# Row loads, first-layer entry and side-job steps rearranged in a trunk kernel with pooled gMLP mixer and 7-product MLP

## Chip, cores, metric

One Trainium2 chip, all 8 NeuronCores; every core runs the same program on its own eighth of the tokens, with no exchange between cores. The metric is the device time of the slowest core, in microseconds. Cores 0 to 3 are one die, 4 to 7 the other.

## What is computed

For each token row `x` (width 1024, float32 in memory): `h = RMSNorm(x)*g1`; `z = h @ w_in` (1536 columns: 512 pooling, 512 `u`, 512 `v`); pooling mixer: trailing means over 2, 4, 8 or 16 tokens minus the token, then a 128x128 map per group and a scale; gMLP mixer: `gelu(u) * (W_s gelu(v) + b)` over chunks of 128 tokens; `x += [pool | gmlp] @ w_out`; `x += relu(RMSNorm(x)*g2 @ w_up)**2 @ w_down` with 4096 hidden columns; a final RMSNorm gives `y`. Small outputs are the last pooling rows and `v` of the sample chunk. Each core has 33 tiles of 128 token rows, and 16 halo rows in front.

## The kernel before

**Tiles and groups.** The 33 tiles form nine groups (`GROUPS`, L18): group 0 has 3 tiles, group 1 has 2, groups 2 to 8 have 4. A ring of nine slots `XS` holds the float32 rows; tile t of the core lies in slot t mod 9. So the rows of group i+2 go into slots that rows of group i leave: row 0 of group i+2 into the slot of the last row of group i-1, rows 1, 2 and 3 into those of rows 0, 1 and 2 of group i. A row is loaded by `load_x` (L402 to L405), squared and summed on ACT (`sq`, L349, into `JUNK`), its inverse root taken on POOL (`rs`, L354 to L358), multiplied on DVE into `HB` (`apply`, L361 to L366), transposed on PE (L373) and copied by ACT (L377). At the end `final_sq`, `final_rs` and `final_out` (L770 to L787) do the same for the last norm, and `final_out` stores the row to `yall`.

**Order by hand.** Nothing is reordered by a compiler. `add(engine, ...)` appends to one of five in-order engine programs and works out the semaphore waits (from L49). A DMA is issued from the SP, ACT or POOL program, and an issue whose wait is not yet met holds up everything behind it in that program. Row loads in the middle of the kernel, row stores, the `rs` pairs and the loads and stores of raw MLP weights all stand in the POOL program.

**Stages.** (1) Entry (L790 to L892): rows of groups 0 and 1, `WAU` (four pieces, `w_in` for pooling and u), `WV`, `w_out`, small constants; PE runs 24 spare matmuls (L562), then transposes and projections `WI_au` (L419), `WI_v` (L440). Float32 weights are converted to bf16 on the way in, by DMAs in the POOL program. (2) Two rounds c = 0, 1 of pairs (L909 to L976): groups 0 and 1 go through the MLP with raw weights in a ring of five 1 MB buffers (`RING`); `pair_UP` (L580) is one step each, then step u(k) is the k-th of 20 `pair_DN` steps (L594). Beside them DVE forms weight sums (`wsum`, L602, L608) for the fast products, which are stored to scratch by the SP program, and the four sets of raw weights are stored too. (3) Group 2 (`plain`) has 32 `UP` steps (L619), then 28 DN steps d(0) to d(27) (L757). (4) Groups 3 to 8: the up product as seven half-size products (L668): 23 steps, `US2(0)`, then `US1(b+1)`, `US3(b)` (L705, L709), `US2(b+1)` (L697) in turn; called the UP stage here, with steps 0 to 22; then 28 DN steps. `US3`'s copy on ACT (L705) and its two subtractions on DVE (L709) must be done before PE may write the same banks again, two products later.

**Side jobs.** Each main step has side jobs, appended after it: `side(k, ...)`. The tables `ws`, `e1`, `tn` and `dn` hold their steps. In stage 4, with i the group whose MLP runs and j = i+1: `tn` holds the steps in the UP stage for j's norm (`sq`, `ap`, `tr`), projections (`v`, `au`), pooling (`pl`), the last norm of rows 2 and 3 of group i-1 (`fq`, `fo`) and the load of row 3 of j (`lx`); `dn` holds those in the DN stage, `lx=(3, 22, 25)` among them: row 0 of group i+2 at d(3), and rows 1 and 2 at d(22) and d(25), one step behind the `final_out` of rows 0 and 1 of group i at d(21) and d(24). The loads overwrite the slot that this `final_out` has just given to its store.

Of the kernel before, what the change touches and what calls it, by code (L numbers as in the profile page):

```python
# [117 lines left out]
def build_nc():  # L118
# [36 lines left out]
    with contextlib.ExitStack() as es:  # L155
# [106 lines left out]
        def schedule(P, order, record):  # L262
# [550 lines left out]
            spare(24)  # L813

            sq("1", 3, XH, [("X", 8)], 16)
            rs("1", 3, 4, 16)
            hb_h = next_hb()
            add("dve", lambda e: e.scalar_tensor_tensor(out=HB[hb_h][0:16], in0=XH, scalar=RS["1"][0:16, 3:4], in1=G1B[0:16],
                                                        op0=ALU.mult, op1=ALU.mult),
                reads=[("X", 8), ("RS", "1", 3), "G1B"], writes=[("HB", hb_h)])  # L820
            N1_sq(0, 0)
            rs("1", 0, 1)
            N1_apply(0, 0)
            norm_T(HB[hb_h], [("HB", hb_h)], HT[:, :, 0:16], ["HMh"], 16)
            for n in range(1, 3):
                N1_sq(0, n)
                rs("1", n, n + 1)
                N1_apply(0, n)
                N1_T(0, n - 1)
# [313 lines left out]
```

How the kernel before makes its waits and increments, by code:

```python
        def run(engname, e, final=False):  # L77
            waited = {}
            pe_ch = prog.engchan["pe"]
            for fn, waits, chn in prog.ops[engname]:
                need = {}
                for w in waits:
                    if engname == "pe" and w.chan is pe_ch:
                        continue
                    if w.val > need.get(w.chan, 0):
                        need[w.chan] = w.val
                for ch, v in need.items():
                    if waited.get(ch, 0) >= v:
                        continue
                    e.wait_ge(ch.sem, v)
                    waited[ch] = v
                ins = fn(e)
                ins.then_inc(chn.sem, chn.inc)
            if final:
                for ev in final_waits:
                    e.wait_ge(ev.chan.sem, ev.val)
```

## Time and profile before

| what | us |
|---|---|
| median of 3 runs | 1239.54 (1237.45 to 1247.37) |
| the profiled execution, own time | 1246.71 |
| its slowest core (1), first to last instruction | 1245.2 |
| its spans over the 8 cores | 1212.4 to 1245.2 |
| PE matmul busy on core 1 | 1179.2 |

The profiled execution is one execution with all cores recorded; 1.5 us of its time lie outside the span. Its own time is 7.2 us above the median of the other three. Times in timeline rows run from the first instruction of that core. A timeline row gives start, length, engine, line, operation, names, and in brackets how long the engine sat idle before it and what ended that.

### The profile page before, as it was taken

What the parts mean: (1) busy time and instruction counts of PE and PEld (TensorE: products, weight loads), DVE (VectorE), ACT (ScalarE), POOL (GpSimd) and SP (SyncE); (2) the same over time, 40 slices, a digit from 0 to 9 for tenths busy, and PEclk for the clock granted to TensorE, in tenths of its full rate; (3) what the DMA queues carried; (4) which work ended last, traced back from release to release, by engine and by line L of the source; (5) the groups of instructions that cost most, each with busy time, mean ns of one, the idle gap of its engine ahead of it and who ended that gap; (6) DMA issues with size and microseconds to landing.
All of it is one profiled execution on the core that took longest, in us unless ns stands there. A gap on an engine that the chain in (4) does not pass through costs nothing.

```text
span 1245.2 us, 21470 instructions; the slowest of 8 cores (1212.4 to 1245.2 us)
## 1 busy us (share of the span) xinstructions
PE 1179.2 (95%) x7412; PEld 701.2 (56%) x7412; DVE 803.9 (65%) x1164; ACT 438.2 (35%) x678; POOL 156.8 (13%) x303
## 2 busy tenths in 40 slices
PE   6889999988999999999999999997999999999996
PEld 2547456533444577446754577445764576547842
DVE  3564545386567675867587675865778575976773
ACT  3446022323410454134530364132640365233401
POOL 3111000113000220022100220021100220011001
PEclk7999999999899989999999999998999999999998
DMA  9996798989995895769767794769856896869993
GB/s 197 167 212 168 210 249 208 209 327 311 331 310 196 261 311 176 255 228 314 270 228 235 263 332 165 267 217 305 281 199 224 252 371 135 299 201 324 307 330 130
DMA packets 64907, 310.41 MB, mean 249 GB/s; under 512 B 9872, under 2 KB 9936, under 8 KB 44064
## 3 DMA queue, kind: packets, MB, share of 16 engines
q1 hardware_dynamic: 48992, 239.35, 57.9%
q0 software_dynamic: 15664, 69.15, 21.8%
q8 instruction: 62, 1.02, 0.3%
q10 hardware_dynamic: 144, 0.52, 0.2%
q14 instruction: 45, 0.37, 0.1%
HBM read 277.90 MB, written 53.31 MB: 266 GB/s over the span
## 4 chain that ended last, share of the span: by engine, by line
PE 73%; DMA 17%; DVE 3%; issue 3%; ACT 2%; POOL 1%; DVEq 0%; POOLq 0%; SPq 0%; ACTq 0%
PE ps L757 23%; PE ps L668 20%; PE ps L538 9%; PE ps L419 9%; DMA scr_up<-RING 5%; DMA yall<-XS 5%; PE ps L440 4%; PE ps L619 3%; PE ps L594 3%; DMA RING<-w_mlp 2%; DMA RING<-scr_up 2%; PE ps L373 2%; DMA XS<-xall 1%; ACT JUNK L350 1%; DMA scr_um<-RING 1%
## 5 line engine op out<-in xcount | busy, mean ns | idle before, releaser
L757 PE MATMUL ps<-RING,ST 128*128 128x512 bf16 x1120 | 256.9, 379 | 0.3 <-DVE ST L730 0.3
L350 ACT ACTIVATE JUNK<-XS 128x1024 bf16<-128x1024 f32 (+1 forms) x100 | 105.5, 1055 | 315.3 <-DVE XS L543 228.9
L668 PE MATMUL ps<-H2T,RING 128*128 128x256 bf16 x1536 | 184.1, 278 | 16.6 <-DVE ST L709 15.0
L757 PEld LDWEIGHTS ps<-RING,ST 128*128 128x128 bf16 x1120 | 108.7, 98 | 126.5 <-issue 1.7
L668 PEld LDWEIGHTS ps<-H2T,RING 128*128 128x128 bf16 x1536 | 152.2, 100 | 47.8 <-issue 20.1
L767 DVE TENSOR_TENSOR XS<-XS,ps 128x512 f32<-128x512 f32 x140 | 95.8, 685 | 75.3 <-PE ps L757 70.8
L668 PE MATMUL ps<-SB,RING 128*128 128x256 bf16 x1152 | 138.8, 273 | 3.9 <-DMA RING<-scr_um 2.2
L668 PEld LDWEIGHTS ps<-SB,RING 128*128 128x128 bf16 x1152 | 111.3, 98 | 20.4 <-issue 5.6
L719 ACT ACTIVATE ST<-ST 128x1024 bf16<-128x1024 bf16 x96 | 101.4, 1056 | 54.9 <-DVE ST L709 50.5
L419 PE MATMUL ps<-HT,WAU 128*128 128x512 bf16 (+2 forms) x512 | 118.0, 379 | 1.4 <-ACT HT L377 1.4
L709 DVE TENSOR_TENSOR ST<-PQ,ps 128x512 bf16<-128x512 f32 x96 | 61.7, 684 | 64.7 <-ACT PQ L705 37.5
L757 PE MATMUL ps<-RING,SB 128*128 128x512 bf16 x448 | 101.4, 379 | 0.0
L357 POOL TENSOR_SCALAR SS<-SS 128x1 f32<-128x1 f32 (+1 forms) x66 | 20.9, 317 | 607.8 <-ACT JUNK L350 606.5
L419 PEld LDWEIGHTS ps<-HT,WAU 128*128 128x128 bf16 x512 | 50.7, 99 | 55.1 <-issue 4.4
L543 DVE TENSOR_TENSOR XS<-ps,XS 128x512 f32<-128x512 f32 x66 | 45.4, 688 | 46.4 <-PE ps L538 44.7
L594 PE MATMUL ps<-RING,ST 128*128 128x512 bf16 x320 | 73.2, 385 | 1.4 <-DVE XS L599 1.4
L697 DVE TENSOR_TENSOR ST<-ps,PQ 128x512 bf16<-128x512 f32 x96 | 63.2, 686 | 15.1 <-PE ps L668 15.1
L757 PEld LDWEIGHTS ps<-RING,SB 128*128 128x128 bf16 x448 | 43.1, 98 | 48.3
L619 PE MATMUL ps<-H2T,RING 128*128 128x512 bf16 x256 | 58.4, 390 | 6.7 <-DMA RING<-scr_up 6.7
L783 DVE SCALAR_TENSOR_TENSOR XS<-XS,RSf,GFB 128x1024 f32<-128x1024 f32 (+1 forms) x34 | 42.1, 1249 | 26.7 <-POOL RSf L358 26.7
L705 ACT ACTIVATE PQ<-ps 128x512 f32<-128x512 f32 x48 | 28.7, 597 | 85.3 <-PE ps L668 75.1
L714 DVE SCALAR_TENSOR_TENSOR ST<-ST 128x1024 bf16<-128x1024 bf16 x48 | 58.4, 1216 | 0.0
(107 smaller groups left out, 1421.6 us busy)
## 6 DMA issues: line engine op xcount, KB each, us to landing
RING<-scr_dn SPq DMA_DIRECT2D x98, 1024.0 KB, 6.3
RING<-scr_um SPq DMA_DIRECT2D x120, 512.0 KB, 7.8
RING<-scr_up SPq DMA_DIRECT2D x48, 512.0 KB, 8.9
RING<-w_mlp POOLq DMA_DIRECT2D x16, 1024.0 KB, 14.8
yall<-XS POOLq DMA_DIRECT2D x29, 512.0 KB, 8.4
RING<-scr_wo SPq DMA_DIRECT2D x14, 1024.0 KB, 5.8
XS<-xall POOLq DMA_DIRECT2D x24, 512.0 KB, 7.9
scr_up<-RING POOLq DMA_DIRECT2D x8, 1024.0 KB, 14.1
```

Source lines behind the costliest of these rows:

```text
L350: add("act", lambda e: e.activation(out=JUNK[0:np_], in_=ap, func=AF.Square, scale=1.0 / 32, accum_out=SS[kind][0:np_, j:j + 1]), reads=re ...
L419: i_ = e.matmul(bank(fb)[:, 0:h0 + T], lhsT=WAU[:, m, k, :], rhs=rhs, start=(k == 0), stop=(k == 7))
L538: i_ = e.matmul(bank(fb)[:, :], lhsT=mix(i, k, n * 128, (n + 1) * 128), rhs=W[:, k, :], start=(k == 0), stop=(k == 7))
L594: i_ = e.matmul(bank(ub)[:, :], lhsT=HID[h](j0 + kk, n * 128, (n + 1) * 128), rhs=RING[s][:, kk, :], start=(kk == 0), stop=(kk == 7))
L619: i_ = e.matmul(bank(ub)[:, :], lhsT=RING[s][:, k, (m % 4) * 128:(m % 4 + 1) * 128], rhs=H2T[:, k, :], start=(k == 0), stop=(k == 7))
L668: i_ = e.matmul(bank(ub)[:, u * 256:(u + 1) * 256], lhsT=RING[s][:, h * 4 + k, c0 + u * 128:c0 + (u + 1) * 128], rhs=op[:, k, :], start=(f ...
L697: add("dve", lambda e, o=o, pb=pb: e.tensor_tensor(out=o, in0=v2(bank(pb)), in1=v2(PQ[b % 2][:, 0:512]), op=ALU.subtract), reads=[("PQ", b ...
L709: add("dve", lambda e, o=o, pb=pb: e.tensor_tensor(out=o, in0=v2(PQ[b % 2][:, 0:512]), in1=v2(bank(pb)), op=ALU.subtract), reads=[("PQ", b ...
L714: add("dve", lambda e: e.scalar_tensor_tensor(out=ST[:, m:m + 2, :], in0=ST[:, m:m + 2, :], scalar=0.0, in1=ST[:, m:m + 2, :], op0=ALU.max ...
L719: add("act", lambda e, fn=fn: e.activation(out=ST[:, m2:m2 + 2, :], in_=ST[:, m2:m2 + 2, :], func=fn), writes=st_res(m2 * 512, (m2 + 2) * ...
L757: i_ = e.matmul(bank(ub)[:, :], lhsT=lh(kk), rhs=RING[s][:, kk, :], start=(c == 0 and kk == 0 and M not in CONT), stop=(c == 1 and kk == 7 ...
L767: add("dve", lambda e, x=x, op_=op_: e.tensor_tensor(out=x, in0=x, in1=bank(ub)[:, :], op=op_), writes=[("BANK", ub), xres(i, rb * 2 + n)])
```

## The change

1. Entry. The first `WAU` piece waits for row 0 of group 0 instead of the halo rows, and stands behind the halo's `rs` in the POOL program; the other three pieces stand behind the `rs` of row 0. The three squares of group 0 go in front of all transposes and copies in the ACT program. The loads of group 1's two rows wait for `WAU` piece 2 (tensor rows m = 2, 3) instead of row 2 of group 0; `PSC`, and behind it in the SP program `PWF`, `BB` and `G2B`, waits for the last piece.
2. Pairs. Weight sum 4 from u(12) to u(11), weight sum 3 from u(14) to u(16), with the release of their ring buffers, in both rounds; the transposes of group 2's second norm one step earlier, u(4, 5, 7, 8).
3. Group 2's UP stage: the square of row 2 of group 3 from step 19 to 21. (`us=` in the new table is read nowhere, and `lx=(8, ...)` gives the old step.)
4. Groups 3 to 8: rows 1, 2 and 3 of group j are loaded in the UP stage at steps 1, 3 and 7; before, rows 1 and 2 at d(22) and d(25) of the DN stage before it, and row 3 at step 6. The `gate` jobs move from d(5, 5, 7, 7) to d(4, 4, 6, 6).

```diff
-            for m in (0, 2, 4, 6):
-                add("pool", lambda e, m=m: e.dma_start(out=WAU[:, m:m + 2], in_=w_au[:, m:m + 2]),
-                    reads=[("X", 8)] if m == 0 else [], writes=[("WAU", m), ("WAU", m + 1)], dma=f"wau{m}")
+            def load_au(m, lead):
+                add("pool", lambda e: e.dma_start(out=WAU[:, m:m + 2], in_=w_au[:, m:m + 2]),
+                    reads=lead, writes=[("WAU", m), ("WAU", m + 1)], dma=f"wau{m}")
...
+            sq("1", 3, XH, [("X", 8)], 16)
+            rs("1", 3, 4, 16)
+            load_au(0, [("X", 0)])
...
+            for n in range(3):
+                N1_sq(0, n)
+            rs("1", 0, 1)
+            for m in (2, 4, 6):
+                load_au(m, [])
+            N1_apply(0, 0)
+            norm_T(HB[hb_h], [("HB", hb_h)], HT[:, :, 0:16], ["HMh"], 16)
+            for n in range(1, 3):
+                rs("1", n, n + 1)
+                N1_apply(0, n)
+                N1_T(0, n - 1)
             for n in range(2):
                 add("sp", lambda e, n=n: e.dma_start(out=xap(1, n), in_=xall[(3 + n) * 128:(4 + n) * 128, :]),
-                    reads=[("X", 2)], writes=[xres(1, n)], dma=f"xldsp{slot_x(1, n)}")
-            add("sp", lambda e: e.dma_start(out=PSC[:], in_=pool_scale[:, :]), writes=["PSC"], dma="su5")
+                    reads=[("WAU", 2)], writes=[xres(1, n)], dma=f"xldsp{slot_x(1, n)}")
+            add("sp", lambda e: e.dma_start(out=PSC[:], in_=pool_scale[:, :]), reads=[("WAU", 6)], writes=["PSC"], dma="su5")
...
-                ws = dict(w=(5, 6, 10, 12, 14))
+                ws = dict(w=(5, 6, 10, 11, 16))
...
-                    e1 = dict(... na=(2, 3, 4, 5), nt=(5, 6, 8, 9), ...)
+                    e1 = dict(... na=(2, 3, 4, 5), nt=(4, 5, 7, 8), ...)
...
-                        side(8, L(load_x, j, n))
-                    tn = dict(sq=(15, 17, 19, 21), ...)
+                        side(tn["lx"][n], L(load_x, j, n))
+                    tn = dict(sq=(15, 17, 21, 21), ... us=(7, 7, 7, 7), lx=(8, 8, 8, 8))
...
-                    tn = dict(... fq=(0, 0), fo=(1, 7), lx=6)
+                    tn = dict(... fq=(0, 0), fo=(1, 7), lx=(1, 3, 7))
...
-                        side(tn["lx"], L(load_x, j, 3))
+                        for n in range(3):
+                            side(tn["lx"][n], L(load_x, j, n + 1))
...
-                dn = dict(... lx=(3, 22, 25), gt=(5, 5, 7, 7), ...)
+                dn = dict(... lx=3, gt=(4, 4, 6, 6), ...)
...
-                        side(d(dn["lx"][0]), L(load_x, i + 2, 0))
+                        side(d(dn["lx"]), L(load_x, i + 2, 0))
...
-                        if i + 2 < NG:
-                            side(d(dn["lx"][1 + n]), L(load_x, i + 2, n + 1))
```

## Rows read from the trace of the kernel before

**Rows 1.** The page: head and busy time by engine.
```profile
span 1245.2 us, 21470 instructions; the slowest of 8 cores (1212.4 to 1245.2 us)
PE 1179.2 (95%) x7412; PEld 701.2 (56%) x7412; DVE 803.9 (65%) x1164; ACT 438.2 (35%) x678; POOL 156.8 (13%) x303
```

**Rows 2.** Spans and mean granted clock of three of the cores.
```profile
core 1: 1245.2 us, clock 0.979
...
core 3: 1232.9 us, clock 0.985
...
core 7: 1212.4 us, clock 0.988
```

**Rows 3.** Core 1, five UP stages, one and the sum: length, busy (count), clock, DMA, GB/s.
```profile
844.90:924.90 80.00, 72.99 (x578) 55.61 (x577) 49.57 (x67) 38.70 (x55) 10.26 (x19) 0.96 0.75 253
...
sum 384.90, PE 365.63 PEld 277.43 DVE 249.24 ACT 194.60 POOL 51.40; mean PE 73.13 PEld 55.48 DVE 49.85 ACT 38.92 POOL 10.28
```

**Rows 4.** Core 7: the sum of the same five stages.
```profile
sum 362.20, PE 359.73 PEld 274.68 DVE 249.31 ACT 194.23 POOL 51.48; mean PE 71.95 PEld 54.94 DVE 49.86 ACT 38.85 POOL 10.30
```

**Rows 5.** Core 3: the sum of the same five stages.
```profile
sum 370.10, PE 361.03 PEld 274.15 DVE 249.27 ACT 194.16 POOL 51.53; mean PE 72.21 PEld 54.83 DVE 49.85 ACT 38.83 POOL 10.31
```

**Rows 6.** Core 1, waits of PE from 400 to 1100 us: total, times, longest.
```profile
PE ps L668 <- DVE ST L709: 15.0, 5, 7.0
```

**Rows 7.** Core 7, waits of PE from 400 to 1100 us: the same line.
```profile
PE ps L668 <- DVE ST L709: 0.3, 1, 0.3
```

**Rows 8.** Core 1, timeline of POOL, end of group 5's DN stage.
```profile
837.61 0.63 POOL L786 DMA_DIRECT2D yall<-XS  x1
...
850.23 0.54 POOL L786 DMA_DIRECT2D yall<-XS  x1
861.45 0.53 POOL L404 DMA_DIRECT2D XS<-xall  x1 [10.68 <-DMA yall<-XS]
```

**Rows 9.** Core 1, timeline of DVE and of PE just behind it.
```profile
863.09 1.29 DVE L783 SCALAR_TENSOR_TENSOR XS<-XS,RSf,GFB 128x1024 f32<-128x1024 f32 x1 [7.86 <-POOL RSf L358]
...
865.12 4.93 PE L668 MATMUL ps<-H2T,RING 128*128 128x256 bf16 x32 [7.01 <-DVE ST L709]
```

**Rows 10.** Core 7, timeline of ACT and POOL, the same place.
```profile
835.17 0.63 POOL L786 DMA_DIRECT2D yall<-XS  x1
...
841.43 1.06 ACT L350 ACTIVATE JUNK<-XS 128x1024 bf16<-128x1024 f32 x1
...
846.16 1.05 ACT L350 ACTIVATE JUNK<-XS 128x1024 bf16<-128x1024 f32 x1
```

**Rows 11.** Core 7, row loads issued from 400 to 1100 us, issue to landing.
```profile
DMA to landing us min/median/max: 5.5/9.1/9.8
```

**Rows 12.** Core 1, row stores issued from 400 to 1100 us, issue to landing.
```profile
DMA to landing us min/median/max: 5.9/8.5/11.2
```

**Rows 13.** Core 1, entry: timeline of SP and PE.
```profile
16.84 1.07 SPq L805 DMA_DIRECT2D XS<-xall  x2
...
23.20 7.13 PE L419 MATMUL ps<-HT,WAU 128*128 128x400 bf16 x27 [1.37 <-ACT HT L377]
...
41.17 5.32 PE L419 MATMUL ps<-ST,WAU 128*128 128x256 bf16 x32 [1.26 <-ACT ST L377]
```

**Rows 14.** Core 1, DMA issues from 16.8 to 17.5 us: KB each, median us to landing.
```profile
XS<-xall SPq DMA_DIRECT2D x2, 512.0 KB, 12.4
```

**Rows 15.** Core 1, pieces of the chain that ended last, from 84 to 260 us.
```profile
88.21 16.55 DMA scr_up<-RING
...
156.08 1.73 PE ps L594 x8
```

**Rows 16.** Core 1, timeline of POOL and PE, rounds c = 0 and c = 1.
```profile
180.17 0.53 POOL L307 DMA_DIRECT2D RING<-w_mlp  x1 [8.34 <-DMA scr_dn<-RING]
...
252.64 0.61 PE L373 MATMUL ps<-IDB,HB 128*128 128x128 bf16 x8 [3.75 <-DVE HB L364]
```

**Rows 17.** Core 1, DMA issues from 160 to 162 us.
```profile
scr_dn<-RING SPq DMA_DIRECT2D x1, 1024.0 KB, 18.7
```

More of the change, by code:

```diff
@@ L799, in schedule @@
             add("pool", lambda e: e.dma_start(out=IDB[:], in_=ident[:, :]), writes=["IDB"], dma="su0")
-            for m in (0, 2, 4, 6):
-                add("pool", lambda e, m=m: e.dma_start(out=WAU[:, m:m + 2], in_=w_au[:, m:m + 2]),
-                    reads=[("X", 8)] if m == 0 else [], writes=[("WAU", m), ("WAU", m + 1)], dma=f"wau{m}")
+            def load_au(m, lead):
+                add("pool", lambda e: e.dma_start(out=WAU[:, m:m + 2], in_=w_au[:, m:m + 2]),
+                    reads=lead, writes=[("WAU", m), ("WAU", m + 1)], dma=f"wau{m}")
             add("sp", lambda e: e.dma_start(out=INVC[:], in_=invc[:, :]), writes=["INVC"], dma="su6")
+            spare(24)
+            sq("1", 3, XH, [("X", 8)], 16)
+            rs("1", 3, 4, 16)
+            load_au(0, [("X", 0)])
+            hb_h = next_hb()
+            add("dve", lambda e: e.scalar_tensor_tensor(out=HB[hb_h][0:16], in0=XH, scalar=RS["1"][0:16, 3:4], in1=G1B[0:16],
+                                                        op0=ALU.mult, op1=ALU.mult),
+                reads=[("X", 8), ("RS", "1", 3), "G1B"], writes=[("HB", hb_h)])
+            for n in range(3):
[9 more added lines that the diff above has]
+                N1_T(0, n - 1)
             for n in range(2):
                 add("sp", lambda e, n=n: e.dma_start(out=xap(1, n), in_=xall[(3 + n) * 128:(4 + n) * 128, :]),
-                    reads=[("X", 2)], writes=[xres(1, n)], dma=f"xldsp{slot_x(1, n)}")
-            add("sp", lambda e: e.dma_start(out=PSC[:], in_=pool_scale[:, :]), writes=["PSC"], dma="su5")
+                    reads=[("WAU", 2)], writes=[xres(1, n)], dma=f"xldsp{slot_x(1, n)}")
+            add("sp", lambda e: e.dma_start(out=PSC[:], in_=pool_scale[:, :]), reads=[("WAU", 6)], writes=["PSC"], dma="su5")
             add("sp", lambda e: e.dma_start(out=PWF, in_=pool_wt[:, :, :]), writes=["GFB"], dma="su7")
@@ L812, in schedule @@
             add("sp", lambda e: e.dma_start(out=G2B[:], in_=g2.partition_broadcast(128)), writes=["G2B"], dma="su3")
[L813 to L829, printed above, removed]
             N1_T(0, 2)
@@ L960, in schedule @@
                 else:
-                    e1 = dict(v=(1, 3), pl=(0, 1, 2, 3), gt=(8, 8, 9, 10), wo=(14, 15, 16, 17, 18, 19, 20, 21), nq=(21, 22, 23, 24), rs=(23, 23, 25, 25), na=(2, 3, 4, 5), nt=(5, 6, 8, 9), fq=(16, 17, 18), fo=(19, 19, 19))
+                    e1 = dict(v=(1, 3), pl=(0, 1, 2, 3), gt=(8, 8, 9, 10), wo=(14, 15, 16, 17, 18, 19, 20, 21), nq=(21, 22, 23, 24), rs=(23, 23, 25, 25), na=(2, 3, 4, 5), nt=(4, 5, 7, 8), fq=(16, 17, 18), fo=(19, 19, 19))
                     for n in range(2):
@@ L1005, in schedule @@
                 if plain:
+                    tn = dict(sq=(15, 17, 21, 21), ap=(18, 20, 22, 24), tr=(23, 27, 27, 30), v=(36, 37, 39, 39), au=(31, 31, 33, 34, 35, 36, 37, 38), pl=(34, 36, 38, 39), us=(7, 7, 7, 7), lx=(8, 8, 8, 8))
                     side(0, *[L(final_sq, 1, n) for n in range(2)], L(final_rs, 0, 2))
@@ L1008, in schedule @@
                     for n in range(4):
-                        side(8, L(load_x, j, n))
-                    tn = dict(sq=(15, 17, 19, 21), ap=(18, 20, 22, 24), tr=(23, 27, 27, 30), v=(36, 37, 39, 39), au=(31, 31, 33, 34, 35, 36, 37, 38), pl=(34, 36, 38, 39))
+                        side(tn["lx"][n], L(load_x, j, n))
                 else:
-                    tn = dict(sq=(2, 5, 7, 11), ap=(3, 6, 9, 12), tr=(5, 8, 11, 14), v=(6, 11, 14, 19), au=(15, 16, 18, 18, 20, 21, 23, 24), pl=(18, 18, 21, 22), fq=(0, 0), fo=(1, 7), lx=6)
+                    tn = dict(sq=(2, 5, 7, 11), ap=(3, 6, 9, 12), tr=(5, 8, 11, 14), v=(6, 11, 14, 19), au=(15, 16, 18, 18, 20, 21, 23, 24), pl=(18, 18, 21, 22), fq=(0, 0), fo=(1, 7), lx=(1, 3, 7))
                     for n in (2, 3):
@@ L1016, in schedule @@
                     if j < NG:
-                        side(tn["lx"], L(load_x, j, 3))
+                        for n in range(3):
+                            side(tn["lx"][n], L(load_x, j, n + 1))
                 d = lambda k: d0 + k
-                dn = dict(s1=(0, 1, 2, 3), s7=(5, 5, 8, 9), s2=(10, 10, 11, 11), s6=(11, 11, 13, 12), sm=(12, 12, 13, 13), fq=(18, 20), fo=(21, 24), lx=(3, 22, 25), gt=(5, 5, 7, 7), wo=(10, 11, 12, 13, 14, 15, 16, 17), nq=(14, 15, 16, 17), na=(16, 16, 17, 18), nt=(17, 18, 19, 21), es=(25, 25, 26, 27, 27), u1=25)
+                dn = dict(s1=(0, 1, 2, 3), s7=(5, 5, 8, 9), s2=(10, 10, 11, 11), s6=(11, 11, 13, 12), sm=(12, 12, 13, 13), fq=(18, 20), fo=(21, 24), lx=3, gt=(4, 4, 6, 6), wo=(10, 11, 12, 13, 14, 15, 16, 17), nq=(14, 15, 16, 17), na=(16, 16, 17, 18), nt=(17, 18, 19, 21), es=(25, 25, 26, 27, 27), u1=25)
                 if plain:
```

## The prediction

> **What bounds the kernel now.** I read the page first: PE is busy 1179.2 of 1245.2 us on the slowest core [rows 1]. So only two things can move the time: the roughly 66 us in which PE has no matmul, and the speed of the matmuls. The spans by core come next: the same program takes 1212.4 us on core 7 and 1245.2 on core 1 [rows 2]. The metric is the slowest core, so I ask where cores 1 and 7 part. A table by stretches gives it: the five UP stages of groups 3 to 7 sum to 384.9 us on core 1, 362.2 on core 7 and 370.1 on core 3 [rows 3 to 5]. That is 22.7 us of the 32.8 between cores 1 and 7, and 7.9 for core 3. The last ten arise before group 2's DN stage ends.
>
> The waits of PE in that part name the place: 15.0 us in 5 times on core 1, one per stage, for DVE's subtraction L709; 0.3 us on core 7 [rows 6, 7]. 22.7 is more than 15.0 because a long wait also costs clock: the worst stage (80.0 us) has a mean granted clock of 0.96 against the full 2.4 GHz [rows 3].
>
> The timelines give the chain behind it. POOL issues row 0's store at 837.61. The only instruction between this and row 1's store is the load of row 1, which overwrites the slot being stored, and row 1's store goes out only at 850.23. The next load stands 10.68 us for that store, until 861.45 [rows 8]. Behind these in POOL's program stand the inverse roots of the last norm of rows 2 and 3. DVE waits 7.86 us for them, starts that multiplication at 863.09, and only then comes L709, for which PE waited 7.01 us, to 865.12 [rows 9]. Stores take 8.5 us in the median and up to 11.2 [rows 12]; two in series decide whether the roots come late. A core with quick DMAs slips through, one with slow ones stalls.
>
> **The change part by part.**
>
> (a) Row loads out of d(22) and d(25). In the new order POOL issues both stores, the four small instructions of two roots, row 2's store, and only then the load of row 1; its slot's store is then some 18 us old, so nothing is waited for. The double wait goes from all five boundaries. Gain on core 1: its sum comes down to core 7's, at most 22.7 us; on core 3 at most 7.9. What is late next is the row itself. On core 7 row 2's store went out at 835.17, so row 1's load goes out 0.6 us behind, or up to 2 us earlier since its root was itself held back: 834 to 836. With the median landing of 9.1 us [rows 11] the row is there at 843 to 845. Its square stood at 841.43 [rows 10]: ACT now waits 2 to 3.5 us. Row 2's load goes one root pair later, 836 to 837.5, lands at 845 to 847, and its square stood at 846.16 [rows 10]: about in time. Row 3's load moves behind one more step and one more store in POOL's program and keeps four steps, as row 1 has; I price it like row 1. Behind a waiting square on ACT stand two passes of the squared ReLU, the evacuation of `V` and the next `US` copy; behind its root on DVE the next `PQ` sum. PE needs these banks only two products later. From below the cost is nothing (all slack). From above it is the whole lateness, 3.5 twice, times 1.5 for the clock (22.7 over 15.0, [rows 3, 4, 6]): 10.5 us per boundary. I take 1.3, near the lower end, as a copy held 1 to 1.5 us still meets the bank in time and core 7 took similar shifts with 0.3 us of PE wait [rows 7]. Five boundaries: +6.5 us on every core.
>
> (b) Entry. Row 2 of group 0 arrives at 16.8 us on core 1 (the SP issue at 16.84 waited for it), and projections start at 23.20 [rows 13]. Without weights beside them the rows should come by 12 to 13, the three squares run without a transpose copy between them, and projections start near 18.5: 4 to 5 us earlier. Three DMA issues of 0.5 us now stand in front of the second root, inside this. But the loads of group 1's rows leave not at 16.84 but when the second weight piece lands, about 20, and take 12.4 us in the median of the pair [rows 14], the second longer. So that row comes near 35, and with square, root, multiply, transposes and copies of 1 to 1.3 us each the second projection block starts near 40.5 against 41.17 [rows 13], on quick cores perhaps 0.5 us later. What is won is given back. And both sit before a DMA chain: the first scratch store of raw weights takes 16.55 us, 88.21 to 104.8 [rows 15], since it stands behind a backlog of weights, whose volume the change leaves alone. If all 4.7 us survived it would be -4.7; if the second row is late and lets PE cool, +2. I take 0.
>
> The Trainium skill (DMA: Bandwidth & Descriptors, section Issuing engines are not separate DMA queues) says that DMAs of all issuing engines run on the same 16 engines and interleave. By that rule, splitting or delaying pieces changes only who is served first and the entry's sum stays 0, as taken; no run here shows it yet.
>
> (c) Weight sums. Sum 4 goes one step forward, sum 3 two steps back, which with the projections between them is up to 7 us of PE work (four times 8 matmuls of 1.73 us, [rows 15]). In round 0 sum 3's store is on the chain: POOL's load at 180.17 waits 8.34 us for it [rows 16], and the store takes 18.7 us [rows 17]. It takes that long because it stands behind two earlier megabytes in SP's queue, which drain whether it is issued at 161 or 168. So 0 to 2 us, up to 7 if it isn't so; I take 0.5, within (d)'s rounding. DVE work is the same, in another place.
>
> (d) Transposes at u(4, 5, 7, 8). In round 1 PE stands 3.75 us at the fourth transpose, until 252.64, for a product on DVE that stands behind a weight sum waiting for a raw load [rows 16]. That load is set by DMA. One step earlier PE meets the same late operand with one pair step (8 matmuls, 1.73 us [rows 15]) more still to do. Cost 1.7 us, from below 0 on a core where the load is early. Taken +1.7 on all cores.
>
> (e) Square at step 21 in group 2, and the gates one step earlier in DN: the same instructions in another order, in DN stages whose length did not differ between cores; DVE's gate work (eight passes of 0.7 us) lies beside PE's DN matmuls. If that cover failed it would be a microsecond per group. Taken 0.
>
> **Sum.** Against the profiled execution: core 1 gives 1245.2 - 22.7 + 6.5 + 1.7 = 1230.7; core 3 gives 1232.9 - 7.9 + 6.5 + 1.7 = 1233.2, and becomes the slowest. Plus 1.5 us outside the span: 1234.7, 12 us under 1246.7. But the profiled execution was 7.2 us above the median of the three runs, and part of that is surely the very stall that goes. I give half of it to the stall and half to the rest, so the forecast stands 3.3 us under 1234.7: 1231.4, 0.7% under 1239.54.
>
> **Rivals.**
> - The new waits take the place of the old: the late rows hold ACT, then DVE, then PE in each of five boundaries, on all cores alike, quick ones too. For it: a landing of 9.1 us against about 7 us of room. Against: two products of slack. It decides against the change from 3.7 us per boundary on (core 3: 1225.0 + 1.7 + 5 x 3.7 = 1245.2). At 6 us: 1225.0 + 1.7 + 30 + 1.5 = 1258, against the median about 1254. Slower.
> - The slack covers the rows entirely and the entry's gain survives: 1231.4 - 6.5 - 2 = 1223. For it: core 7 shows that lateness of 1 to 2 us is swallowed. Against: the DMA chain behind the entry.
> - Sum 3's later store shifts the raw-weight chain by its whole 7 us: 1231.4 + 7 = 1238, no measurable change. For it: the load waits for exactly that store. Against: the queue in front of it.
> - The change does not reach the slowest core, because some core is slow by ring loads and clock, not by this stall, in most runs: 1239.
>
> **How the numbers follow.** Forecast 0.50 (own range 1226 to 1237), new waits 0.13, chain shift 0.12, all slack 0.20, not reached 0.05. A measurement here tells about 1% from no change: 1227.1 and 1251.9. Faster by over 1%: most of the slack case and a tenth of the forecast, 0.25. Slower: the new waits beyond 5 us per boundary (0.08) and what I have not seen (0.02), 0.10. The rest 0.65. The range, 1222 to 1243, leaves out the heavy end of the new waits and little else.
>
> **What would show it right or wrong.** Right: no POOL wait at row loads from 400 us on, PE's wait for L709 near 0 to 1 us per boundary on every core, ACT waits of 1 to 3 us at the squares of rows 1 and 3, UP stages of 73 to 74 us on all cores, cores closer together. In the entry: projections at 18 to 19 us, then a PE gap before the second block near 40 us. The fourth transpose of round 1 waits 5 to 6 us. Wrong: UP stages of 76 us and more on core 7 (new waits), a load after sum 3's store later than 182 us, or an equal spread of the cores as before.

## The result, and the profile after the change

The changed kernel takes 1249.21 us in the median of 19 runs, the kernel before, run beside it, 1239.54 in the median of 19. The ratio is 1.0082, 95% interval 1.0065 to 1.0100: slower by 0.8%, where 0.7% faster was forecast, and above the range of 1222 to 1243. Some executions of either kernel are much slower, with a lower granted clock on one die; the ratio leaves them out, so it isn't quite the quotient of the medians. The profiled execution took 1252.26 us, 5.5 more than that of before.

The page of the profile after, cut to the head, PE's busy time and the chain that ended last (by line):

```profile
span 1250.7 us, 21476 instructions; the slowest of 8 cores (1234.2 to 1250.7 us)
...
PE 1179.1 (94%) x7412; PEld 699.9 (56%) x7412; DVE 803.7 (64%) x1164; ACT 437.5 (35%) x678; POOL 152.7 (12%) x303
...
PE ps L757 26%; PE ps L668 17%; PE ps L538 8%; PE ps L419 8%; DMA XS<-xall 4%; PE ps L594 4%; DMA scr_up<-RING 4%; PE ps L619 3%; PE ps L440 3%; DMA RING<-scr_um 3%; PE ps L580 3%; PE ps L373 2%; DMA RING<-w_mlp 2%; DMA scr_dn<-RING 1%; DMA scr_um<-RING 1%
```

PE's busy time is what it was [rows 1]. What is new is a 4% share of `XS<-xall` in the chain: landings of row loads now stand on it. Spans and mean granted clock of the fastest core and of the slowest:

```profile
core 3: 1234.2 us, clock 0.982
...
core 6: 1250.7 us, clock 0.979
```

Before they ran from 1212.4 to 1245.2 [rows 2]. The cores are closer, as forecast, but they met at the slow end: the quickest lost 21.8 us and the slowest lost 5.5.

The waits say that the edit did what it was for. First POOL's waits on core 1, then PE's on core 0 and on core 7, then ACT's for row landings on core 0, all from 400 to 1100 us (what waited, for what: total, times, longest):

```profile
POOL SS L357 <- ACT JUNK L350: 484.9, 34, 73.1
POOL yall L786 <- DVE XS L783: 72.3, 15, 7.0
...
PE ps L373 <- DVE HB L364: 5.0, 5, 1.7
PE ps L668 <- DVE PQ L681: 4.4, 7, 0.9
PE ps L668 <- DVE ST L709: 0.4, 1, 0.4
...
PE ps L373 <- DVE HB L364: 7.6, 7, 2.2
PE ps L668 <- DVE PQ L681: 5.5, 9, 0.9
...
ACT JUNK L350 <- DMA XS<-xall: 27.8, 9, 4.5
```

POOL stands before no row load any more, on any core, and PE's wait for L709, 15.0 us on core 1 before [rows 6], is gone from core 1 and 0.4 us on core 0. In its place PE waits for `HB` (L364, the product of group j's first norm) and for `PQ` (L681), also on core 7, which had 0.3 us of the old wait [rows 7]. `HB` waits on the rows: ACT stands 27.8 us in nine times for landings, a wait that no core had before.

The five UP stages of groups 3 to 7, one stage and the sum on core 0 and the sum on core 6, in the columns of [rows 3]:

```profile
696.50:772.40 75.90, 73.72 (x578) 55.78 (x577) 49.63 (x67) 38.60 (x55) 9.62 (x19) 0.98 0.78 257
...
sum 377.60, PE 366.07 PEld 276.62 DVE 249.54 ACT 194.04 POOL 45.71; mean PE 73.21 PEld 55.32 DVE 49.91 ACT 38.81 POOL 9.14
...
sum 382.90, PE 365.32 PEld 275.62 DVE 249.24 ACT 193.93 POOL 45.67; mean PE 73.06 PEld 55.12 DVE 49.85 ACT 38.79 POOL 9.13
```

All eight cores lie between 377.6 and 384.2 us. Before they lay between 362.2 and 385.0, so only the slowest is no worse off. Averaged over the eight cores, with the same rule of cutting for every kernel (first to last L668 product of a stage), the five stages went from 373.1 to 381.0 us, and the start of the first of them from 416.4 to 421.0. Both carry scatter: of the 17 kernels of this document seven have the row loads of before and lie between 372.3 and 377.5, and seven have the front of before and start the first of these stages between 416.4 and 420.0.

**One stage, row by row.** POOL on core 0, in the stage that begins at 696.5:

```profile
708.61 0.63 POOL L786 DMA_DIRECT2D yall<-XS  x1 [3.42 <-DVE XS L783]
709.24 0.53 POOL L404 DMA_DIRECT2D XS<-xall  x1
...
710.84 0.62 POOL L404 DMA_DIRECT2D XS<-xall  x1
721.52 0.22 POOL L357 TENSOR_SCALAR SS<-SS 128x1 f32<-128x1 f32 x1 [10.06 <-ACT JUNK L350]
```

The load of row 1 goes out behind row 2's store, 12.7 us into the stage, that of row 2 1.6 us later. The landing times of these two (min/median/max of two issues):

```profile
DMA to landing us min/median/max: 10.8/11.4/12.1
```

So 10.8 us for row 1 and 12.1 for row 2. The forecast had taken 9.1, the median of before [rows 11]. ACT, DVE and PE of core 0 behind it:

```profile
720.20 1.06 ACT L350 ACTIVATE JUNK<-XS 128x1024 bf16<-128x1024 f32 x1 [4.27 <-DMA XS<-xall]
...
721.26 2.19 ACT L719 ACTIVATE ST<-ST 128x1024 bf16<-128x1024 bf16 x2
723.35 0.58 ACT L445 ACTIVATE V<-ps 128x512 bf16<-128x512 f32 x1
723.83 0.59 ACT L679 ACTIVATE PQ<-ps 128x512 f32<-128x512 f32 x1
...
722.56 1.28 DVE L364 SCALAR_TENSOR_TENSOR HB<-XS,RS,G1B 128x1024 bf16<-128x1024 f32 x1 [3.76 <-POOL RS L358]
724.52 0.69 DVE L681 TENSOR_TENSOR PQ<-ps,PQ 128x512 f32<-128x512 f32 x1 [0.67 <-ACT PQ L679]
...
723.99 0.61 PE L373 MATMUL ps<-IDB,HB 128*128 128x128 bf16 x8 [1.42 <-DVE HB L364]
725.36 2.99 PE L668 MATMUL ps<-SB,RING 128*128 128x256 bf16 x16 [0.76 <-DVE PQ L681]
```

The row is 4.27 us late for its square. PE first stands 1.42 us for the transpose of this very row, then 0.76 for the `PQ` sum, which is late by the four ACT instructions that stood behind the square. Right behind these two gaps the granted clock falls to half. The window from 725.4 to 729.4 (length, busy, clock in the third column from the right):

```profile
725.40:729.40 4.00, 4.00 (x22) 2.97 (x23) 3.74 (x6) 3.07 (x5) 1.95 (x4) 0.58 0.84 272
```

Four microseconds at 0.58 lose 4.00 x 0.42 = 1.7 us. With the gaps that is 1.42 + 0.76 + 1.7 = 3.9 us, and this stage is 75.9 us where a stage of core 7 before took 362.2 / 5 = 72.4 [rows 4]: 3.5 more.

### The profile page after: what moved, and what is told of

Read it like the earlier page. It is cut to its first block, busy times and chain, and to the rows that moved or that the text cites. A ratio compares the mean times of both kernels' runs of the same rounds, so it can differ in the third digit from the quotient of the medians.

```text
span 1250.7 us, 21476 instructions; the slowest of 8 cores (1234.2 to 1250.7 us)
## 1 busy us (share of the span) xinstructions
PE 1179.1 (94%) x7412; PEld 699.9 (56%) x7412; DVE 803.7 (64%) x1164; ACT 437.5 (35%) x678; POOL 152.7 (12%) x303
## 4 chain that ended last, share of the span: by engine, by line
PE 75%; DMA 16%; DVE 3%; issue 2%; ACT 2%; POOL 1%; DVEq 0%; POOLq 0%; ACTq 0%; SPq 0%
PE ps L757 26%; PE ps L668 17%; PE ps L538 8%; PE ps L419 8%; DMA XS<-xall 4%; PE ps L594 4%; DMA scr_up<-RING 4%; PE ps L619 3%; PE ps L440 3%; DMA RING<-scr_um 3%; PE ps L580 3%; PE ps L373 2%; DMA RING<-w_mlp 2%; DMA scr_dn<-RING 1%; DMA scr_um<-RING 1%
## 5 line engine op out<-in xcount | busy, mean ns | idle before, releaser
L350 ACT ACTIVATE JUNK<-XS 128x1024 bf16<-128x1024 f32 (+1 forms) x100 | 105.5, 1055 | 354.7 <-DVE XS L543 228.9
L668 PE MATMUL ps<-H2T,RING 128*128 128x256 bf16 x1536 | 178.8, 273 | 1.5 <-DVE ST L697 1.4
L668 PEld LDWEIGHTS ps<-H2T,RING 128*128 128x128 bf16 x1536 | 149.6, 98 | 30.2 <-issue 5.0
L668 PE MATMUL ps<-SB,RING 128*128 128x256 bf16 x1152 | 141.1, 275 | 9.2 <-DVE PQ L681 5.3
L668 PEld LDWEIGHTS ps<-SB,RING 128*128 128x128 bf16 x1152 | 112.0, 99 | 28.3 <-issue 12.7
L709 DVE TENSOR_TENSOR ST<-PQ,ps 128x512 bf16<-128x512 f32 x96 | 61.6, 683 | 57.2 <-PE ps L668 32.4
L373 PE MATMUL ps<-IDB,HB 128*128 128x128 bf16 (+1 forms) x536 | 42.2, 224 | 32.1 <-DVE HB L364 32.1
L364 DVE SCALAR_TENSOR_TENSOR HB<-XS,RS,G1B 128x1024 bf16<-128x1024 f32 x33 | 42.3, 1281 | 46.5 <-POOL RS L358 46.5
L697 DVE TENSOR_TENSOR ST<-ps,PQ 128x512 bf16<-128x512 f32 x96 | 63.2, 685 | 12.7 <-PE ps L668 12.4
L373 PEld LDWEIGHTS ps<-IDB,HB 128*128 128x128 bf16 (+1 forms) x536 | 35.5, 100 | 46.1 <-issue 36.6
## 6 DMA issues: line engine op xcount, KB each, us to landing
RING<-w_mlp POOLq DMA_DIRECT2D x16, 1024.0 KB, 15.6
```

The source lines that it names most:

```text
L350: add("act", lambda e: e.activation(out=JUNK[0:np_], in_=ap, func=AF.Square, scale=1.0 / 32, accum_out=SS[kind][0:np_, j:j + 1]), reads=re ...
L373: i_ = e.transpose(out=bankbf(fb)[:, k * 128:k * 128 + np_], in_=src[0:np_, k * 128:(k + 1) * 128], identity=IDB[0:np_, 0:np_])
L668: i_ = e.matmul(bank(ub)[:, u * 256:(u + 1) * 256], lhsT=RING[s][:, h * 4 + k, c0 + u * 128:c0 + (u + 1) * 128], rhs=op[:, k, :], start=(f ...
L697: add("dve", lambda e, o=o, pb=pb: e.tensor_tensor(out=o, in0=v2(bank(pb)), in1=v2(PQ[b % 2][:, 0:512]), op=ALU.subtract), reads=[("PQ", b ...
L709: add("dve", lambda e, o=o, pb=pb: e.tensor_tensor(out=o, in0=v2(PQ[b % 2][:, 0:512]), in1=v2(bank(pb)), op=ALU.subtract), reads=[("PQ", b ...
```

## The experiments

Each kernel below was timed against the kernel before on the same chip: e1 to e4 share one chip, e5 to e8 a second, e9 to e12 a third and e13 to e15 a fourth. "UP sum" is the sum of the five UP stages, mean over the eight cores of the run's one profiled execution. It is 373.1 before and 381.0 after.

**Only the row loads (e1), and all but the row loads (e2).**

```diff
# e1, against before; e2 takes the same lines back out of the changed kernel
-                    tn = dict(... fo=(1, 7), lx=6)
+                    tn = dict(... fo=(1, 7), lx=(1, 3, 7))
-                dn = dict(... lx=(3, 22, 25), ...)
+                dn = dict(... lx=3, ...)
```

> The kernel before with only the row loads of groups 3 to 8 moved (steps 1, 3 and 7). Theory A (late rows hold ACT, DVE and PE in each of five UP stages): the five stages sum to 377 to 383 us on every core, as in the changed kernel (377.6 on its quickest core, 362.2 on the quickest of before), no wait of PE for the subtraction L709; time 1.000 to 1.006 of before, since the slowest core trades one stall for the other. Rival B (the loss is in the first 420 us alone, the row loads are a gain): the slowest core drops by 10 us, ratio 0.990 to 0.995.

> The changed kernel with the row loads of groups 3 to 8 back at d(22), d(25) and step 6. Theory A: UP sums spread again from 362 to 385 us, the first UP stage starts near 421 us in the mean as in the changed kernel (416 before), time 1.002 to 1.006 of before: part of the loss stays, since it comes from entry and pairs. Rival B: all of the loss stays or more, 1.010 and above.

e1: 1249.86 against 1243.86, ratio 1.0048 (1.0027 to 1.0069). UP sum 381.0, on all cores between 377.2 and 385.6: the whole loss in these stages comes from the row loads. PE and ACT on core 0 of e1, 400 to 1100 us:

```profile
PE ps L373 <- DVE HB L364: 6.3, 5, 2.1
PE ps L668 <- DVE PQ L681: 5.2, 9, 0.9
...
ACT JUNK L350 <- DMA XS<-xall: 30.0, 9, 5.1
```

e2: 1.0068 (1.0038 to 1.0097). UP sum 372.3, between 362.9 and 380.9: the old pattern with the old stall, which core 1 of e2 shows (PE, then POOL):

```profile
PE ps L668 <- DVE ST L709: 11.4, 4, 7.8
...
POOL XS L404 <- DMA yall<-XS: 57.3, 10, 12.2
```

So with the row loads as they were the kernel is slower than before too, a little more than I expected (1.002 to 1.006): there is a second loss, ahead of 420 us.

**Only the entry (e3), only the pairs (e4).** e3 has point 1 of the change alone, e4 point 2 alone (`w=(5, 6, 10, 11, 16)` and `nt=(4, 5, 7, 8)`).

```diff
# e4
-                ws = dict(w=(5, 6, 10, 12, 14))
+                ws = dict(w=(5, 6, 10, 11, 16))
-                    e1 = dict(... nt=(5, 6, 8, 9), ...)
+                    e1 = dict(... nt=(4, 5, 7, 8), ...)
```

> The kernel before with only the new entry. If the entry is the source of the later start (second projection block 41.5 instead of 39.3 us in the mean, first pair step 86.5 instead of 83.9): first pair step 2 to 3 us later and the first UP stage as much later, 418 to 419 us in the mean, ratio 1.001 to 1.003. If the DMA chain behind it absorbs it, as I had forecast: first UP stage at 416 to 417, ratio 0.999 to 1.001.

> The kernel before with only the weight sums and the second-norm transposes of the pair rounds moved. If only the transpose costs (forecast 1.7 us): the fourth transpose waits 3.2 to 5.5 us instead of 1.4 to 3.8, first UP stage at 418 in the mean. If the later store of weight sum 3 also delays the chain of raw loads: that transpose waits 5 us and more on most cores and the first UP stage starts at 419 to 421. Ratio 1.001 to 1.004.

e3: 1.0014 (0.9982 to 1.0046). e4: 1.0018 (1.0000 to 1.0036). Neither is told from no change. Their first UP stage starts at 418.5 and 419.0 us, as expected, but kernels with the front of before reach 420.0, so this mark decides nothing. With e1 the three add up to 1.0080, which is the whole change, though the intervals are too wide for the sum to prove much.

**Row loads earlier instead (e5), consumers later instead (e8).** Both take rows 1 and 2 out of the DN stage as the change does. e5 puts their loads at step 0, right behind the two roots and ahead of row 2's store; e8 keeps the change's steps and moves what uses the rows one step back.

```diff
# e5, against before (dn as in e1)
+                    tn = dict(... fo=(1, 7), lx=(0, 0, 6))
# e8, against before (dn as in e1)
-                    tn = dict(sq=(2, 5, 7, 11), ap=(3, 6, 9, 12), tr=(5, 8, 11, 14), v=(6, 11, 14, 19), ...)
+                    tn = dict(sq=(2, 6, 8, 12), ap=(3, 7, 10, 13), tr=(5, 9, 12, 14), v=(6, 12, 14, 19), ... lx=(1, 3, 7))
```

> The kernel before with rows 1 and 2 loaded at step 0 of the UP stage, behind the last norm's two inverse roots and ahead of row 2's store, row 3 at step 6 as before. Theory A: what hurts is only how late the rows' loads go out; here they go out 4 to 6 us earlier than in the changed kernel and the roots still don't stand behind a store. The five UP stages sum to 361 to 368 us on every core, ACT waits under 1 us at a row's square, slowest core 8 to 12 us less, ratio 0.990 to 0.994. Rival C (a row load in the UP stage collides with the ring loads and PE waits for the ring, wherever it stands): sum 372 and more, ratio 0.998 to 1.004.

> The moved row loads alone (steps 1, 3, 7), but the squares of rows 1, 2 and 3 one step later (6, 8, 12) with their products and transposes behind them. Theory A: the wait is for the landing, so each step given to it takes 1.7 to 2.6 us off ACT's wait of 4.3 us; UP sums fall from 381 to 364 to 372 us on every core, ratio 0.993 to 1.000. Rival C: sums stay near 381.

e5: 1241.58 against 1248.62, ratio 0.9945 (0.9927 to 0.9964), UP sum 369.3 (364.5 to 372.6). e8: 0.9969 (0.9950 to 0.9988), UP sum 373.7. In both PE's wait for L709 is gone as in the change, and both are faster than before. What differs from e1 is how long the row has until its consumer. The stages of core 0 in e5, one and the sum:

```profile
692.30:764.90 72.60, 71.74 (x570) 54.89 (x577) 49.47 (x67) 38.66 (x55) 9.54 (x19) 1.00 0.84 272
...
sum 364.40, PE 358.28 PEld 274.53 DVE 249.00 ACT 194.11 POOL 48.49; mean PE 71.66 PEld 54.91 DVE 49.80 ACT 38.82 POOL 9.70
```

POOL and PE of that stage, and in a second fence the longest wait of PE and ACT's wait for landings from 400 to 1100 us, same core:

```profile
700.98 1.16 POOL L404 DMA_DIRECT2D XS<-xall  x2
704.46 0.54 POOL L786 DMA_DIRECT2D yall<-XS  x1 [2.32 <-DVE XS L783]
...
718.52 0.61 PE L373 MATMUL ps<-IDB,HB 128*128 128x128 bf16 x8
718.97 1.91 PE L668 MATMUL ps<-SB,RING 128*128 128x256 bf16 x16
```

```profile
PE ps L668 <- DMA RING<-scr_um: 3.0, 5, 0.9
...
ACT JUNK L350 <- DMA XS<-xall: 0.8, 1, 0.8
```

The first load goes out 8.7 us into the stage instead of 12.7. These 4.0 us remove both of PE's gaps and with them the half clock (1.00 in the stage, 0.98 after).

It isn't all of the forecast, though: the UP sum was to be 361 to 368 us on every core, and core 0 is one of three that reach that. On core 2 (371.8 us) PE waits for ring loads instead, from 400 to 1100 us:

```profile
PE ps L668 <- DMA RING<-scr_up: 4.0, 3, 1.6
PE ps L668 <- DMA RING<-scr_um: 2.9, 7, 0.7
```

In the mean over the cores these ring waits are 3.7 us before, 1.7 after and 6.1 in e5, and all waits of PE in that part 10.8, 14.7 and 8.0. So the rival of this run, that row loads in the UP stage make PE wait for the ring, may hold for a part: when nothing else is late, the ring loads are. Whether the row loads delay them was not tried. POOL also stands again before a row load in e5, chiefly row 3's at step 6, for row 2's store (11.9 to 20.0 us per core); in e14 below, with step 7, it doesn't, and the UP sum is no better for it.

In e8 core 0's wait for `HB` falls to 1.5 us, but that for `PQ` stays, and the UP sum of 373.7 stays above the 364 to 372 expected:

```profile
PE ps L668 <- DVE PQ L681: 4.2, 6, 0.9
PE ps L373 <- DVE HB L364: 1.5, 4, 0.5
...
ACT JUNK L350 <- DMA XS<-xall: 8.3, 6, 2.5
```

**The two edits of the pairs apart (e6, e7).**

```diff
# e6
+                    e1 = dict(... nt=(4, 5, 7, 8), ...)
# e7
+                ws = dict(w=(5, 6, 10, 11, 16))
```

> The kernel before with only the transposes at u(4, 5, 7, 8). Forecast of the step: +1.7 us at the fourth transpose, first UP stage at 418 us in the mean, ratio 1.001 to 1.002.

> The kernel before with only weight sums 3 and 4 moved. If the queue in front of the store hides its later issue: first UP stage at 416 to 417 us, ratio 0.999 to 1.001. If the raw loads behind it are delayed: first UP stage at 418 and more, ratio 1.001 to 1.003.

e6: 1.0004 (0.9987 to 1.0021). e7: 1.0007 (0.9983 to 1.0031). No verdict from the times; their traces say more, below.

**The changed kernel with rows at step 0, whole and without one part of the front.**

```diff
# e10, against the changed kernel; e11 also has w=(5, 6, 10, 12, 14), e12 also the old entry
-                    tn = dict(... lx=(1, 3, 7))
+                    tn = dict(... lx=(0, 0, 6))
```

> The changed kernel with its row loads at steps 0, 0 and 6. If the parts add up (row loads so placed 0.9945 alone, the rest of the change 1.0068 alone): 1.000 to 1.003. UP sums 364 to 373 us, first UP stage near 421 us in the mean.

> The same with the weight sums back at u(12) and u(14). If the later weight sum is what costs in the first 420 us together with the new entry: the first UP stage 2 to 4 us earlier than in the run beside it, ratio 0.995 to 0.999. If the weight sums are free: no difference.

> The same as the first of the three with the old entry. If the entry costs only together with the later weight sum, or is the larger part: first UP stage 2 to 3 us earlier than with the new entry, ratio 0.995 to 0.999. If the DMA chain hides the entry's 3 us: no difference from the first of the three.

e10: 1244.78 against 1249.48, 0.9964 (0.9942 to 0.9987), UP sum 368.5. Three step numbers take the changed kernel from 1.0082 to 0.9964, from the slow side of the kernel before to the fast one, and further than I expected (1.000 to 1.003). e11: 0.9955 (0.9938 to 0.9972), e12: 0.9957 (0.9936 to 0.9979). Putting back the weight sums or the entry moves the ratio by 0.1% at most, inside every interval, and the first UP stage from 423.6 us to 422.6 and 422.1, where 2 us or more were expected.

**The entry with group 1's rows let go early (e9).**

```diff
# e9, against e3
-                    reads=[("WAU", 2)], writes=[xres(1, n)], dma=f"xldsp{slot_x(1, n)}")
+                    reads=[("X", 2)], writes=[xres(1, n)], dma=f"xldsp{slot_x(1, n)}")
```

> The new entry alone, but group 1's rows released by row 2 of group 0 as before (near 11 us instead of 19). If their late release is what makes the second projection block late (PE waits of 2 to 3 and 3.5 to 4.6 us for them): that block starts at 37 to 39 us instead of 41.8, the first pair step at 83 to 84. If they then hold up the weight pieces instead: projections start later than 19.5 us or stop in between.

e9: 1.0017 (0.9988 to 1.0045). The second projection block starts at 38.3 us in the mean instead of 41.8 in e3, but the first pair step at 88.3 instead of 86.8. The 3.5 us are not only lost again, the sign turns. The trace shows where, DVE and PE on core 5:

```profile
57.06 0.57 DVE L516 TENSOR_TENSOR ps<-ps,BB 128x384 f32<-128x384 f32 x1 [7.52 <-DMA BB<-gmlp_b]
...
58.43 5.25 PE L440 MATMUL ps<-WV,ST 128*128 128x512 bf16 x16 [4.33 <-DVE ST L525]
```

With group 1's rows let go early the bias `BB` lands late: its load stands behind `PSC`, which waits for the last `WAU` piece. DVE waits 5.3 to 8.7 us for it on all eight cores, PE behind it 1.8 to 8.3 us; in e3 neither wait exists on any core.

**Other steps for the loads (e15, e13, e14), each against before.**

```diff
# e15, e13, e14 (dn as in e1)
+                    tn = dict(... lx=(2, 4, 8))
+                    tn = dict(... lx=(1, 3, 6))
+                    tn = dict(... lx=(0, 0, 7))
```

> The kernel before with rows 1, 2 and 3 loaded at steps 2, 4 and 8, one step later still than in the changed kernel. In POOL's program row 1's load then stands behind the root of row 0, 1.6 us later at the most. If cost follows lateness: UP sums rise from 381 to 388 to 395 us on every core, ratio 1.010 to 1.018. If a fixed cost of loading in the UP stage is at work: near 381 and 1.005.

> The kernel before with rows 1 and 2 at steps 1 and 3 and row 3 at step 6 as before. If row 1 carries the cost (ACT waits 4 to 5 us for it): UP sums 377 to 381 us, ratio 1.001 to 1.005. If row 3 carries half of it, as I had priced: sums 370 to 373, ratio 0.996 to 1.000.

> The kernel before with rows 1 and 2 at step 0 and row 3 at step 7, behind the last store. If row 1 carries the cost: UP sums 368 to 372 us as with steps 0, 0, 6 (369.3), ratio 0.993 to 0.997. If row 3 carries half: sums 374 to 377, ratio 0.998 to 1.001.

e15: 1.0006 (0.9977 to 1.0035), UP sum 382.0. e13: 1.0004 (0.9980 to 1.0029), UP sum 378.9. e14: 1242.37 against 1248.54, 0.9928 (0.9896 to 0.9960), UP sum 370.3, the best of all.

e15 was meant as a larger dose and is none. In its stage that begins at 695.4 on core 0 POOL shows:

```profile
707.48 0.62 POOL L786 DMA_DIRECT2D yall<-XS  x1 [3.42 <-DVE XS L783]
708.11 0.54 POOL L404 DMA_DIRECT2D XS<-xall  x1
709.71 0.61 POOL L404 DMA_DIRECT2D XS<-xall  x1
```

Row 1's load goes out 12.7 us into the stage, as with step 1. POOL does not keep PE's steps: it runs its program as fast as its waits allow, and between steps 1 and 2 nothing in it waits. What counts is the place among POOL's instructions. The only border that matters is row 2's store, which waits 3.42 us for DVE: step 0 is ahead of it, steps 1 and 2 are behind.

e13 has row 3's load one step earlier than e1 and its UP sum is 2.1 us less; e14 against e5 has it one step later, with 1.0 us more. So row 3 is worth no more than kernels with the same row loads differ by (372.3 to 377.5), rows 1 and 2 about ten (381.0 or 378.9 against 370.3 or 369.3). In e14 ACT still waits for row 3, 13.7 us per core, and PE next to nothing for `HB` (0.2 us on core 0): that row does have most of the slack I had given to all of them. Most and not all: on five cores PE waits 1.4 to 4.3 us for a square (L350).

The ratios of kernels with steps 1 and 3 are 1.0048, 1.0006 and 1.0004 on two chips. Their UP sums agree within 3.1 us and the intervals just overlap, so a ratio here carries a few tenths of a per cent that differ by chip; the sizes below rest on the stages, not on such differences.

**The front, from all 17 traces.** The times could not tell the parts of the front apart. The traces say more, since stretches between two marks repeat within 1 to 3 us from kernel to kernel. I took five for each kernel, mean over eight cores, and sorted the 17 kernels (before, after, fifteen experiments) by whether they have the edit:

| stretch | without the edit | with it | difference |
|---|---|---|---|
| entry: start to the sixth load of raw weights in POOL | 106.1 (11 kernels; 105.0 to 107.4) | 107.4 (6; 105.9 to 109.1) | +1.3 |
| from there to the tenth such load | 62.6 (11; 61.6 to 63.4) | 62.1 (6; 61.5 to 63.0) | -0.6 |
| weight sum 3 at u(16): tenth to eleventh such load | 9.5 (11; 8.7 to 10.1) | 11.4 (6; 9.3 to 12.4) | +1.8 |
| transposes early: last such load to group 2's first UP | 40.7 (10; 40.1 to 41.4) | 43.0 (7; 42.7 to 43.7) | +2.3 |
| the same: from there to group 3's UP stage | 148.4 (10; 148.0 to 148.9) | 147.3 (7; 146.7 to 147.8) | -1.1 |

From the eleventh load to the last it is 50.5 to 51.7 us in all 17: that chain hands on what it gets. Together 1.3 - 0.6 + 1.8 + 2.3 - 1.1 = 3.7 us. The second row is sorted by the weight sums' edit, as the third is. The entry's ranges overlap, but on the two chips that have kernels of both kinds the difference is +1.5 and +1.4. In the third row e4 is the exception: it has the edit and 9.3 us. Measured directly, group 3's UP stage starts at 422.5 in the mean of after, e2 and e10, which have the whole front, and at 418.6 in the seven with the front of before: 3.9 us.

**The mean over the cores, all timed runs.** The metric takes the slowest core, and its distance from the mean of the eight wanders: from 7.4 to 15.6 us in runs of the kernel before on one chip. The mean itself is steadier, so I took it over the 5 to 11 runs of each kernel that its ratio rests on, less that of before on the same chip (1230.6 to 1233.9); the standard error of such a difference is 0.4 to 0.8 us:

| kernel | mean over cores, to before | slowest core above that mean |
|---|---|---|
| before | 0 | 10.9 to 13.5 |
| e1 rows / e15 / e13 | +8.2 / +7.3 / +4.6 | 8.6 / 7.3 / 9.3 |
| e5 / e14, rows at step 0 | -4.6 / -4.7 | 10.4 / 9.6 |
| e8, consumers later | 0.0 | 8.7 |
| e2, all but rows | +5.9 | 13.1 |
| e3 entry / e9 | +2.2 / +1.8 | 11.9 / 12.5 |
| e4 pairs / e6 / e7 | +3.5 / +1.3 / +0.1 | 10.1 / 12.3 / 12.9 |
| e10 / e11 / e12 | -0.9 / -2.3 / -2.1 | 10.5 / 10.1 / 10.0 |

This is the change in one view: row loads at steps 1 and 3 cost the average core 5 to 8 us and bring the slowest 2 to 6 us closer to it (in the changed kernel's own runs it stands 7.4 us above the mean); at step 0 the average core gains and the slowest comes closer as well. It also prices the front once more, e10 less e5: -0.9 + 4.6 = 3.7 us.

## Why the prediction was wrong, step by step

**(a) The old stall: right in its cause, its worth too high.** I took the double wait of POOL as the cause of what slow cores lose, up to 22.7 us on core 1 [rows 3, 4]. e5 and e14 take it away, and no core of e5 is above 372.6 us. But I let every core come down to core 7's 362.2, and e5 stands at 369.3 in the mean: with the stall gone PE waits 6.1 us for ring loads, and 1.1 on core 7 of before.

**(a) The new row waits: the step that failed.** I wrote "I take 1.3, near the lower end, as a copy held 1 to 1.5 us still meets the bank in time". Measured against core 7 of before, as the forecast was, the mean of e1 and of after gives (381.0 - 362.2) / 5 = 3.8 us per boundary, for 1.3. Against e5, which has the same edit with the rows in time, it is (381.0 - 369.3) / 5 = 2.3: so much is won back by bringing the rows in time, and most of the rest is ring waits. The upper bound of 10.5 held. Three things were mis-sized or left out:

- The landing. I took the median of 9.1 us [rows 11]; it was 10.8 and 12.1 for rows 1 and 2 at their new place, where two row loads, a store and three ring loads go out from 707 to 713 us (11.1 and 12.6 in the median of all cores and stages). The lateness became 4.27 us, where 2 to 3.5 were forecast. By the Trainium skill (DMA: Bandwidth & Descriptors, section Issuing engines are not separate DMA queues) the DMAs of all issuing engines interleave on the same 16. The trace agrees: POOL's row loads took 10.8 and 12.1 us beside SP's ring loads, and that rule speaks against taking a landing time from a less crowded place.
- The consumer. I followed the late square only to the banks that PE needs "two products later". But the row has a nearer consumer on PE itself: its own transpose at step 8, behind `HB` at step 6. PE waited there first, 5.0 to 9.1 us per core over the stages. "Two products of slack" was true of the banks and not of the row.
- The clock. The two gaps are followed by a stretch at half speed, 1.7 of 3.9 us. I had such a factor (1.5) only in the upper bound.

The rival "the new waits take the place of the old" is what happened, at 3.8 us per boundary, just past the 3.7 that I had worked out as its turning point. I gave it 0.13 because I read core 7's 0.3 us of wait as proof of slack. That core showed that slack exists for what was late there, not for a row that is 4 us late.

**(b) Entry: nearly right.** The forecast was projections near 18.5, the second block near 40.5 and nothing gained. PE on core 1, after:

```profile
19.53 13.35 PE L419 MATMUL ps<-HT,WAU 128*128 128x400 bf16 x64 [1.37 <-ACT HT L377]
34.97 0.98 PE L373 MATMUL ps<-IDB,HB 128*128 128x128 bf16 x8 [2.09 <-DVE HB L364]
39.62 1.01 PE L373 MATMUL ps<-IDB,HB 128*128 128x128 bf16 x8 [3.68 <-DVE HB L364]
41.90 5.29 PE L419 MATMUL ps<-ST,WAU 128*128 128x256 bf16 x32 [1.26 <-ACT ST L377]
```

The first block starts 3.7 us earlier than before (19.53, a microsecond behind the forecast), the second 0.7 later [rows 13], and the two waits between are those of group 1's late rows. The chain of raw weights starts 1.3 us later (table): inside the bounds of -4.7 to +2, taken as 0. e3's ratio of 1.0014 is not told from nothing; its mean over the cores is 2.2 us up.

**(c) Weight sums: term probably too small.** Taken 0.5 within 0 to 7; the table says 1.8 less 0.6, so 1.2, though e4 shows none of it and e7's mean over the cores is up by only 0.1. On core 1, POOL and SP after:

```profile
182.88 0.53 POOL L307 DMA_DIRECT2D RING<-w_mlp  x1 [12.57 <-DVE ST L586]
...
171.37 0.32 SPq L328 DMA_DIRECT2D scr_dn<-RING  x1
```

The store goes out near 171 instead of near 161 [rows 17], but the load behind it at 182.88 instead of 180.17 [rows 16]: 2.7 us for 10, and 1.7 of the 2.7 were there at the sixth load (107.06 for 105.37). So the argument (the store stands behind two earlier megabytes anyway) held for most of it. The mark I had set, a load later than 182 us, was met on this core.

**(d) Transposes: right.** Taken +1.7, measured +2.3 up to group 2's UP stage, of which 1.1 comes back inside group 2. **(e) Gates and square: right.** From group 3's stage on, all that is not UP stage takes 384.8 to 384.9 us in before, after and e2.

**The sum again.** From forecast to result are 17.8 us. 5 x (3.8 - 1.3) = 12.5 of them are the row term. The front came to 3.9 where about 1.7 to 2.2 were put in: 2 more. These are means over the cores; for the slowest core of the profiled execution nothing is left over. The forecast stood on core 3 with a UP sum of 362.2 + 6.5 = 368.7 and a rest of 1232.9 - 370.1 + 1.7 = 864.5 us. Core 6 of after has 382.9 and 1250.7 - 382.9 = 867.8: 14.2 and 3.3 more, 17.5 together. That a single core's rest differs by 3.3 is front and scatter of the cores, which one execution can't part. The step from the profiled execution to the median was right, 3.3 us for 3.05 measured, but by luck: half of 7.2 is 3.6, and it was to hold a stall that the new waits replaced.

What stays open is the size of the front. e10 against e11 and e12 gives 1.4 and 1.2 us for the weight sums and the entry, the stretches 1.2 and 1.3. On the first chip e3 and e4 add up (2.2 + 3.5 = 5.7) to e2's 5.9, but that is 2 more than e10 less e5 and than the stretches, and e6 and e7 together give 1.4 where e4, which has both edits, gives 3.5. In the ratios no single part of the front is told from zero. And why PE's `PQ` wait in e8 did not go with the `HB` wait was not tried.

## What to carry to other kernels

A load that overwrites a slot must stand behind the short jobs that others wait for, and no further: here the right place was between two roots and the next store (0.9945 and 0.9928), and one place later in the same program turned that into a loss. Follow a late operand to its nearest consumer on the bounding engine, its own product or transpose, and not only to the bank that comes next; and take its landing time under the traffic of the new place. Where the metric is the slowest of eight cores, a repair that helps the slow ones and costs the quick ones nearly 4 us per stage is no repair: look at the quick cores for the price.
